# Attention in a transformer layer: sums of squares and normalisation moved to GpSimd, every step one head further behind

## The reference

```python
    scores = jnp.einsum('bnqkgd,bnskd->bnkgqs', qb, kc).astype(jnp.float32) * SCALE
    logits = jnp.where(valid[None, :, None, None], scores + bias, NEG)
    m = jnp.maximum(jnp.max(logits, axis=-1, keepdims=True), sink)
    e = jnp.exp(logits - m)
    p = e / (jnp.sum(e, axis=-1, keepdims=True) + jnp.exp(sink - m))
    out = jnp.einsum('bnkgqs,bnskd->bnqkgd', p.astype(v.dtype), vc)
...
        y = jnp.concatenate([rmsnorm(y_a, swa_out_g[l]), rmsnorm(y_b, moba_out_g[l])], axis=-1) @ w_o[l]
        x = x + g1 * y
        h = rmsnorm(x, norm2_g[l]) * (1 + sc2) + sh2
        x = x + g2 * hier_moe(h, w_group[l], b_group[l], w_expert_router[l], b_expert_router[l],
                              w_gate[l], w_up[l], w_down[l])
```

## Time and profile before

| | us |
|---|---|
| median of 3 timed runs | 1587.67 |
| lowest and highest | 1583.69, 1589.61 |
| the profiled execution: its own time | 1578.84 |
| its span from first to last instruction | 1577.0 |
| PE busy | 1352.5 (86%) |
| DVE busy | 652.7 (41%) |
| ACT busy | 139.0 (9%) |
| POOL busy | 48.2 (3%) |
| mean granted clock of PE, share of 2.4 GHz | 0.941 |

### The profile page before, as it was taken

One profiled execution on the slowest core, in us unless ns is written; L12 is line 12 of the kernel. 1 busy time (PEld: TensorE's weight loads), 2 busy tenths in 40 slices (PEclk: granted clock), 3 DMA queues, 4 the chain that ended last, 5 costly groups with the idle time before them and its releaser, 6 DMA issues.

```text
span 1577.0 us, 14567 instructions
## 1 busy us (share of the span) xinstructions
PE 1352.5 (86%) x5720; PEld 685.3 (43%) x5720; DVE 652.7 (41%) x984; ACT 139.0 (9%) x390; POOL 48.2 (3%) x60
## 2 busy tenths in 40 slices
PE   2699998988898469988988988988988988988985
PEld 2578777666687355332332332322332322332331
DVE  3657675666575632224223223223223223223225
ACT  2110000056200011000000000000000000000001
POOL 0000000000100000000000000000000000000000
PEclk9799999969999689999999999999999999999998
DMA  9989998924498860999999999999999999999992
GB/s 334 397 316 400 397 408 314 335 110 161 146 392 324 320 260 27 393 424 431 424 426 430 424 425 429 424 425 430 424 425 430 425 424 430 424 426 430 423 425 103
DMA packets 96295, 572.10 MB, mean 363 GB/s; under 512 B 6048, under 2 KB 28752, under 8 KB 54400
## 3 DMA queue, kind: packets, MB, share of 16 engines
q1 hardware_dynamic: 94256, 567.64, 88.1%
q0 software_dynamic: 2000, 3.95, 1.0%
HBM read 569.38 MB, written 2.18 MB: 362 GB/s over the span
## 4 chain that ended last, share of the span: by engine, by line
PE 64%; DMA 23%; DVE 8%; issue 3%; ACT 2%; SPq 0%; DVEq 0%; POOL 0%; POOLq 0%; ACTq 0%
PE PS L1287 21%; DMA ring<-in_w_up 16%; PE PS L1308 11%; PE PS L1267 8%; PE PS L1133 8%; PE PS L1212 5%; DMA ring<-in_w_ada 3%; PE PS L1138 3%; DMA ring<-in_w_o 2%; DVE W L770 2%; PE PS L1249 2%; DVE W L741 2%; PE PS L1083 2%; DVE W L1018 1%; PE PS L1183 1%
## 5 line engine op out<-in xcount | busy, mean ns | idle before, releaser
L1287 PE MATMUL PS<-ring,W 128*64 128x512 f32 x1024 | 240.6, 628 | 40.3 <-DMA ring<-in_w_up 40.3
L1308 PE MATMUL PS<-ring,W 128*64 128x512 f32 x1024 | 233.6, 610 | 27.4 <-DVE W L1018 17.6
L1287 PE MATMUL PS<-ring,gysq 128*64 128x512 f32 x1024 | 224.3, 593 | 14.1 <-DMA ring<-in_w_up 10.6
L1133 PE MATMUL PS<-r,ring 128*128 128x256 f32 x768 | 170.8, 385 | 8.4 <-DVE r L780 6.8
L996 DVE TENSOR_TENSOR r<-r,PS 128x512 f32<-128x512 f32 x128 | 87.9, 687 | 204.1 <-PE PS L1267 204.1
L1287 PEld LDWEIGHTS PS<-ring,W 128*64 128x64 f32 x1024 | 81.6, 144 | 193.7 <-issue 193.7
L1133 PEld LDWEIGHTS PS<-r,ring 128*128 128x128 f32 x768 | 148.2, 194 | 31.7 <-DVE r L780 7.6
L770 DVE SCALAR_TENSOR_TENSOR W<-ring,sm,W 128x2048 f32<-128x2048 f32 x60 | 140.8, 2346 | 42.4 <-DMA ring<-in_w_ada 39.6
L1001 DVE TENSOR_SCALAR W<-W 128x256 f32<-128x256 f32 x32 | 22.0, 689 | 304.4 <-ACT W L654 304.4
L1308 PEld LDWEIGHTS PS<-ring,W 128*64 128x64 f32 x1024 | 76.2, 140 | 163.6 <-issue 144.0
L1267 PE MATMUL PS<-W 128*128 128x512 f32 x256 | 128.5, 641 | 21.2 <-DVE W L1018 21.2
(11 more groups left out here) (207 smaller groups left out, 727.7 us busy)
## 6 DMA issues: line engine op xcount, KB each, us to landing
ring<-in_w_gate SPq DMA_DIRECT2D x64, 2048.0 KB, 25.1
ring<-in_w_up SPq DMA_DIRECT2D x64, 2048.0 KB, 26.9
ring<-in_w_down SPq DMA_DIRECT2D x64, 2048.0 KB, 26.2
ring<-in_w_ada SPq DMA_DIRECT2D x32, 2048.0 KB, 15.0
ring<-in_w_qkv SPq DMA_DIRECT2D x17, 2048.0 KB, 14.5
ring<-in_w_ada SPq DMA_DIRECT2D x32, 1024.0 KB, 14.4
ring<-in_w_o SPq DMA_DIRECT2D x8, 2048.0 KB, 15.1
ring<-u_scr SPq DMA_DIRECT2D x2, 2048.0 KB, 20.7
```

Of the source, the lines that this page charges most:

```text
L1133: last = mm(ps[:, sub * T:(sub + 1) * T], w[:, t, (2 * b + sub) * P:(2 * b + sub + 1) * P], hT[:, QT * q + t, :], start=(t == 0), stop=(t ...
L1287: last = mm(PS[64 * j:64 * j + 64, i % 2, :].rearrange("p (m n) -> p m n", m=2), hE[i % 2][:, k], w[:, :, t, 256 * j:256 * j + 256], start ...
L1308: last = mm(PS[64 * q:64 * q + 64, 4 + i2, :], hidT[:, b, 64 * j:64 * j + 64], w[:, b, 512 * ch:512 * ch + 512], start=(j + b == 0), stop= ...
```

## The change

- The logits are negated: queries are scaled by -SCALE, the bias table and the sinks change sign, DVE takes a minimum, and ACT's exponential gets scale=-1. Line 829 falls away.
- DVE's `normalise` is split. `denominators` (sink's part and reciprocal) stays on DVE, two heads behind the logits; the two multiplications go to POOL.
- The transposes run three heads behind the scores, the values start at turn 6, the squares at turn 8. `L` has five buffers.
- The squares of y are added up on POOL (`add_square`): the first pair of each half is written to the total by ACT, the other seven are added. PE sums over the partitions once per half, behind the loop.
- PE no longer waits for `mod_ok` ahead of the loop, and ACT waits for `mod_out` only ahead of the first write to `PT`, behind the fourth exps.
- POOL's loop stands between its sending of the SH2 row and its wait for that DMA.

```diff
             for i, pt_ in enumerate(MADE):
...
+                if pt_ == SH2:
+                    for h in range(NH + 7):
+                        if h < NH:
+                            normalise(h)
+                        if h >= 8 and h % 2 == 0:
+                            add_square((h - 8) // 2)
                 pool.wait_ge(mod_out, 16 * (i + 1))
...
+            def normalise(h):
+
+                pool.wait_ge(rd_ok, h + 1)
+                Lh = Ls[h % NL]
+                nc.gpsimd.tensor_scalar(Lh[:, 0:T], Lh[:, 0:T], rden[:, h, 0:1], None, ALU.mult)
+                nc.gpsimd.tensor_scalar(Lh[:, T:384], Lh[:, T:384], rden[:, h, 1:2], None, ALU.mult).then_inc(pn_ok, 1)
+
+            def add_square(b):
+
+                i, n = divmod(b, KT // 2)
+                if n:
+                    pool.wait_ge(sq_ok, b + 1)
+                    total = ysq[:, i * T:(i + 1) * T]
+                    nc.gpsimd.tensor_tensor(total, total, sq[:, b % 2 * T:(b % 2 + 1) * T], ALU.add).then_inc(ysq_ok, 1)
+                    pool.wait_ge(ysq_ok, b - i)
...
-            act.wait_ge(mod_out, 16 * 2)
             act.wait_ge(small_in, 32)
-            for h in range(NH + 4):
+            for h in range(NH + 7):
                 if h < NH:
                     exps(h)
-                if 2 <= h < NH + 2:
-                    pt_evac(h - 2)
-                if h >= 5 and h % 2 == 1:
-                    squares((h - 5) // 2)
+                if h == 3:
+                    act.wait_ge(mod_out, 16 * 2)
+                if 3 <= h < NH + 3:
+                    pt_evac(h - 3)
+                if h >= 8 and h % 2 == 0:
+                    squares((h - 8) // 2)
...
-            def normalise(h):
+            def denominators(h):
                 dve.wait_ge(p_ok, h + 1)
                 if h < NHA:
                     link(V.tensor_tensor(psum_[:, h, :], psum_[:, h, :], esink[:, h, :], ALU.add))
-                link(V.reciprocal(rden[:, h, :], psum_[:, h, :]))
-                V.tensor_scalar(L[:, h % 4, 0:T], L[:, h % 4, 0:T], rden[:, h, 0:1], None, ALU.mult)
-                V.tensor_scalar(L[:, h % 4, T:384], L[:, h % 4, T:384], rden[:, h, 1:2], None, ALU.mult).then_inc(pn_ok, 1)
+                V.reciprocal(rden[:, h, :], psum_[:, h, :]).then_inc(rd_ok, 1)
...
-            for h in range(NH + 4):
+            for h in range(NH + 6):
                 if h < NH:
                     logits(h)
-                if 1 <= h <= NH:
-                    normalise(h - 1)
-                if h >= 5 and h % 2 == 1:
-                    y_evac((h - 5) // 2)
-            dve.wait_ge(yss_ps, NH // 2)
+                if 2 <= h < NH + 2:
+                    denominators(h - 2)
+                if h >= 7 and h % 2 == 1:
+                    y_evac((h - 7) // 2)
+            dve.wait_ge(yss_ps, 2)
...
-            pe.wait_ge(mod_ok, 2)
-            for h in range(NH + 5):
+            for h in range(NH + 6):
                 if h < NH:
                     scores(h)
-                if 2 <= h < NH + 2:
-                    transpose_p(h - 2)
-                if 4 <= h < NH + 4 and h % 2 == 0:
-                    values((h - 4) // 2)
+                if 3 <= h < NH + 3:
+                    transpose_p(h - 3)
                 if h >= 6 and h % 2 == 0:
-                    square_sums((h - 6) // 2)
+                    values((h - 6) // 2)
+            pe.wait_ge(mod_ok, 2)
+            for i in range(2):
+                pe.wait_ge(sq_ok, KT // 2 * i + 1)
+                pe.wait_ge(ysq_ok, (KT // 2 - 1) * (i + 1))
+                mm(PS[:, 6 + i, 0:T], ones, ysq[:, i * T:(i + 1) * T], start=True, stop=True).then_inc(yss_ps, 1)
```

## The result

The changed kernel takes 1603.94 us (median of 4 runs, 1602.7 to 1605.58) against 1588.64 for the kernel before in the same comparison: ratio 1.0112, 95% interval 1.0074 to 1.0149, or **+15.3 us**. It is slower. The forecast was 1598.5, with a range of 1570 to 1608.

What follows compares the result with a forecast made beforehand. PE's gapless queue at half clock was taken to bound the attention loop. From the 1587.67 us median, +13.3 for the loop staying at the lower clock and -2.5 for the old kernel's later clock return gave 1598.5, range 1570 to 1608.

Steps and rivals of the forecast that it cites:

- The clock: Attention loop: PE's clock falls at the start as before and, without square sums, stays at 0.50 for the whole loop.
- rival 1: Attention loop: the clock returns as before, near 340 us; 11 us faster, 1577; chance 0.18.
- rival 4: Attention loop: the change does nothing, something outside the chain sets the loop's length; 1588; chance 0.02.
- Rival 2: Attention loop: the clock doesn't fall or is back at once; 19 us faster, 1569; chance 0.10.
- N: POOL's two normalising multiplications per head together: taken as 0.7 us, between 0.39 and 2.09; DVE needed about 0.63.
- The addition: POOL's addition of squares in the loop, one per pair: taken as 0.75 us, between 0.26 and 1.05.
- rival 3: Attention loop: POOL's multiplications are slow, above 1.1 us per head at the lower clock; up to 1614; chance 0.10.
- the forecast's case: Attention loop at the lower clock, PE without gaps, 6.30 us per pair instead of 7.45; chance 0.60.
- The start: Ahead of the loop: first transposes at 316.1 us instead of 317.68, the first exponential no longer waiting for a DMA.
- The sum: First transposes to reader of the sums: 94.5 us of PE plus 3.4, ending at 414.0 against 400.72, +13.3 us.
- The correction for the one profiled execution: Whole kernel: the median lay 8.8 us above the profiled run; one pair's later clock return, 2.5 us, was subtracted.
- Costs taken as nothing: Later DMAs behind POOL's loop and the fifth buffer cost nothing; negated logits save DVE work hidden behind PE.

Runs made afterwards that it cites:

- e3: The kernel before with only the additions of squares moved to POOL, PE summing once per half behind the loop: 1603.4 us, ratio 1.01.
- e9: The changed kernel with multiplications back on DVE and square sums back in PE's loop, five heads late, nothing of the loop on POOL: 1577.63 us, ratio 0.9934.
- e11: The changed kernel plus unused 128x512 matmuls at the start and through the whole loop: 1579.42 us, ratio 0.995.
- e8: The changed kernel plus a burst of four unused 128x512 matmuls behind the scores of head 9: 1607.05 us, ratio 1.0114.
- e1: The changed kernel with the two normalising multiplications per head back on DVE, squares still added on POOL: 1597.08 us, ratio 1.0055.
- e2: The changed kernel with the square sums back on PE, one per pair in the loop, multiplications still on POOL: 1611.73 us, ratio 1.0142.
- e5: The changed kernel with multiplications back on DVE and square sums back in PE's loop, (h-8)/2, nothing of the loop on POOL: 1610.07 us, ratio 1.0123.
- e6: The changed kernel with multiplications back on DVE, plus five unused 128x512 matmuls around the loop's start: 1564.5 us, ratio 0.9845.
- e7: The kernel before plus six unused 128x512 matmuls, one ahead of the loop, one behind head 1, four behind head 2: 1580.75 us, ratio 0.9965.

## Why the prediction was right, and where it was off

- **The clock: right, and the whole of the sign.** The fall at the start, no return without the square sum, 0.50 past 410 us; rival 1 (a return near 340) and rival 4 (no effect) did not come. e3 shows it with nothing but the squares moved, e9 by putting them back in the changed order, e11 by holding the clock with unused work. The prediction named a block of PE's work without scores in front of the return; the returns in e8 and e9 have one too, and with the square sums on POOL (the change, e1, e3) none came before the loop's last values, where the scores have run out. But the block with the square sum does not bring the clock back each time: once it passed before, twice in e9, and in e2 it ran without a wait at 364.49 and 372.20 and passed, while the return there, at 406.1, came at the end of one with a wait of 0.06 us inside (402.64 to 406.25). In e5, where nearly every such block was broken by a wait, none came before 426.2. So the square sums on PE make a return in the loop possible, and which block brings it is open; what exactly the chip measures is not shown by these runs.
- **Rival 2.** PE at 30.00 of 30 us, twice in a row, stayed at 0.50 (e3). The Trainium skill ("TensorE: Matmul & The Clock Gate", Part 1) has the transition come soon into sustained matmul activity; for this loop these traces do not agree, and whether it is the scores' 64 partitions that make the difference is not shown. With the clock held, as the rival asks, the changed kernel takes 1579.4 (e11) and not 1569: the rival's pairs of 4.2 and 3.9 lacked 0.83 us of N, which makes 5.03 and 4.73, against 5.01 and 4.69 measured. Only the variants with the multiplications on DVE reach 1562 to 1567.
- **The term that was mis-sized: N.** The prediction took 0.7 us of 0.39 to 2.09, near the lower end, since the operands are small; it measured 1.53. The two shapes differ by 0.32 us for 128 columns, 2.5 ns each, more than the 1.02 ns of a copy, and there is some 0.29 in front of it. The addition was right (0.75 taken, 0.73 measured).
- **So rival 3 came true in part.** Its point of decision, N = 1.1 at the lower level, holds: 1.53 - 1.1 = 0.43 per window pair, measured 6.69 to 6.77 against 6.30; MoBA pairs 6.44. Between the values at 327.55 and those at 406.38 lie 12 pairs, 78.8 us for the 75.6 of the sum: 3.2 more. e1, with pairs of 6.29, 96.3 us from the first transposes to the reader and 1597.08, is the forecast's case as it was written.
- **The start.** Predicted 316.1 for the first transposes, 1.6 earlier than before. Measured from the first scores it is 6.44 us against 7.23, 0.8 earlier; the missing 0.8 is again N.
- **The sum.** First transposes to reader: 97.9 predicted, 103.0 measured. Of these 5.1 us, 0.5 stand ahead of 327.55, the pairs' 3.2 follow, and 1.4 stand behind 406.38, where POOL has the multiplications of three heads and an addition in a row (410.37 to 415.67). The correction for the one profiled execution (8.8 us under the median, one pair of 2.5 given to the clock's return) was a guess that did little harm: +10.8 us predicted on the medians and 5.1 + 0.8 make 16.7, against 15.3 measured.
- **Costs taken as nothing** that stayed nothing: the DMAs behind POOL's loop (5.47 us from reader to output product, as before), and, in pairs that are PE alone in e1, the fifth buffer and the negated logits.

Open: why the two profiled executions differ by another 5.5 us behind the loop, which the medians do not show. Half of it lies in the first 64 matmul instructions of the experts, 16.73 us (from 647.34) against 13.95 (from 624.98): the clock was 0.50 there until 653.0.

## What to carry to other kernels

Taking work off the engine that bounds a stage can cost time when its clock depends on that work: find what ran in front of each rise of the granted clock before removing it. Test such a case with unused matmuls (here five are worth 2.0% in the changed order, e1 to e6, and six 0.35% in the old one, e7), and price GpSimd by measured rows, not by its copies. A reordering (e1, 0.55% slower than before, the squares on POOL) and a held clock in the old order (e7, 0.35% faster) are each worth little here, and together they are 1.5% (e6).

## What the runs showed of the hardware that I had not expected

- PE without a gap for 60 us at 0.50 (e3: 30.00 of 30 us, twice).
- GpSimd's tensor_scalar on 128x256 took 0.925 us and on 128x128 0.605; the same on DVE 0.353 for 256. Its tensor_tensor on 128x256 took 0.726, less than the one-input multiplication.
- The same GpSimd instruction is as long at either PE clock (925 and 924 ns in the change and e11).
- A DVE instruction on two columns took up to 0.727 us instead of 0.156 beside GpSimd's addition (e6). DVE's multiplication of 128x256, with one input besides its scalars, took 0.54 instead of 0.353 twice beside the same addition (335.85 and 339.95).
- PE ran 3.53 us of transposes, values and square sum without a gap at 0.50, and the clock did not rise (e2, 364.49 to 368.02).
